# Two-layer diffusion backbone block: part of layer 0's gated convolution moved into the first attention block, and nine norm steps moved into the side queue

## The chip, the cores and the metric

The kernel runs on the 8 cores of one Trainium2 chip (trn2). Each pair of cores takes one batch item, each core one half of its 4096 positions (the second core of a pair in mirrored order), and every core runs the same program. The metric is the device time in microseconds of the slowest core.

## The reference

Layer 0 computes, from normalised and modulated tokens `xn`, a dense attention and a short gated convolution side by side, then one output projection, a residual add, a second norm and a SwiGLU feed-forward. Layer 1 is of the same build with windowed attention and a pooling mixer, which the change doesn't touch.

```python
q, k, v, gb, gc, u = split(xn @ w_in)                 # 1536, 512, 512, 512, 512, 512 columns
attn = dense_attention(rope(rms(q)), [kc; rope(rms(k))], [vc; v])   # 12 heads, 4352 keys
conv = gb * short_conv(gc * u, conv_w)                # depthwise, 3 taps, centred
y = concat([attn, conv]) @ w_out
h = h + gate1 * y
hn = rms_norm(h) * (1 + scale2) + shift2              # shift, scale, gate: c @ w_mod
h = h + gate2 * ((silu(hn @ w_gate) * (hn @ w_up)) @ w_down)
```

## The kernel before, in words

A core owns 2176 latent tokens and 256 context tokens, in the five token blocks of `QBLK`: blocks 0 to 3 of 512 tokens and block 4 of 384 (128 latent, 256 context; the gc and u products of block 4 take one more column, the neighbour token). The normalised tokens of the blocks lie in SBUF as `xnA[0]` to `xnA[4]`. Activations have features on the partitions, so a product of 128 output features over one block is 16 matmuls of 128x128 weights by up to 512 columns, summed in one PSUM bank.

The program writes out the order of every engine's instructions. `sc.op` appends to an engine's queue, with waits worked out from the slots that an instruction reads and writes; `sc.dma` appends a transfer to a queue (SP for data, POOL for weights); `sc.late` appends a store some operations later. All five queues run in order.

Weights stream through a ring of three slots (`NRING = 3`, `WStream`). The order of tiles is that of the `ws.take` calls. `ws.release` frees a slot, and `pump` then issues the load of the next tile in that order, which waits until TensorE has read the old one. So a tile is loaded when the tile three places ahead of it has been used, and never earlier. A tile of `w_mod` or `w_out` is 16x128x512 (float32 in HBM, bf16 in SBUF, 2048 KB there), one of `w_aux` (128 features of gb, gc and u) 1536 KB.

Layer 0 goes through these steps:

- `stage_a0`: norms, keys and values, then a list of items that `pipe` overlaps: 60 query items and, behind them, the items of `conv_items`. For each of four feature chunks `c` it takes the chunk's `w_aux` tile and makes gc, u (their product goes to the float32 row `zb`) and gb of all five blocks, 15 products; three taps over `zb` on VectorE, times gb, give the convolution, which is stored to `aux_d`. The products go round five PSUM banks; no other work runs beside them. Item `nq + 7` also keeps a `w_out` tile of layer 1: it is loaded through the ring and stored to `wo_d` by SP, and its slot is free after that store.
- `stage_b0`: attention. The query blocks go in the order `ORD[0]` = 0, 1, 2, 4, 3, called places p0 to p4 here. A place has 12 units (one head, 34 key tiles; p3 is built otherwise), a unit 17 groups of two key tiles. For each group `attn_gen` issues an exponential of 128x1024 on ScalarE, two score matmuls of the next group, two matmuls of the group before by the values, and the sums of the exponentials (VectorE adds and 5 matmuls per unit). A place of 512 queries is thus 204 groups.
- Behind each group, `side.weave` takes steps from a side queue. A group gives a credit of `rate` (2.5 times that for two groups of each unit), a step takes the cost that it yields. In p0 the rate is 0.105 and the queue holds `mod_gen` of the parts 2, 3 and 4 of the modulation: 12 tiles of `w_mod`, two steps per tile (a product of 16 matmuls and a copy; 4 float32 selections that the profile shows as 8 matmuls, and VectorE adds). In the places after it the queue holds `wout_gen`, the output projection of the place before (16 output chunks of 16 matmuls, in steps of 4), with `norm2_gen`, the second norm of the place before that (17 steps). Before a place begins, `side.drain` issues all that is left; the drain stands two groups ahead of the new place.
- `wout_last`: the last projection (p4), with nothing beside it. It issues the products of the first four output chunks, as far as the last heads are not needed, then all 17 steps of the norm of p3, then the loads of `hn` for the feed-forward (`load_hn`), then the rest. From step 28 on it takes one step of `xsum_gen` (VectorE sums for the feed-forward's products) per step of its own.
- The feed-forward, by Strassen-Winograd products (lines 1797 and 1944 of the profile).

Which lines are what in the profile: L593 is `mm`, thus every matmul but the feed-forward's; L1147 the exponential; L1150 the adds of exponentials; L610 the copy of a `mod_gen` tile; L671 and L683 the two operations of a norm step; L1412, L1421 and L1472 square, sum and residual add of `wout_gen`; L1700 the helper `tt` of the feed-forward; L195 and L199 every wait and every DMA.

## Time and profile before

| | us |
|---|---|
| Time, median of 3 runs | 6962.02 (6952.61 to 7265.59) |
| Profiled execution, its own time | 6981.62 |
| Its span, first to last instruction, slowest core (7) | 6980.1 |
| Spans of the eight cores | 6909.7 to 6980.1 |
| TensorE busy in that span | 6524.7 (93%) |
| VectorE / ScalarE busy | 3849.2 (55%) / 2389.2 (34%) |
| Convolution stage | about 732 to 933 |
| Places p0, p1, p2, p3, p4 | 933 to 1190, to 1458, to 1712, to 1884, to 2145 |
| Last projection, up to the feed-forward | 2145 to 2228 |

All rows are of core 7, times in microseconds from the start of its span. Busy time is that of instructions that compute; the granted clock (PEclk) is TensorE's, as a share of 2.4 GHz; the DMA share is the mean busy share of the core's 16 DMA engines. An entry in brackets behind a row of the timeline is the idle time of the engine ahead of it and what ended it.

### The profile page before, as it was taken

The numbers are of one execution on the slowest core, as the hardware profiler recorded it, in microseconds if no ns is written. First come the engines' busy times: TensorE is split into PE (matmuls) and PEld (weight loads), VectorE is DVE, ScalarE is ACT, GpSimd is POOL, SyncE is SP. The second block draws the span as 40 slices with busy tenths as digits, with TensorE's granted clock in tenths as the row PEclk, the third lists the DMA queues.
The fourth block names the chain that finished last, engine by engine and source line by source line (L and its number), as shares of the span: only waits on it lengthen the run. The fifth ranks groups of instructions, "written<-read, shape, count | busy, mean of one in ns | idle before, by whom it ended". The sixth has DMA issues, their size and how long they took to land.

```text
span 6980.1 us, 105992 instructions; the slowest of 8 cores (6909.7 to 6980.1 us)
## 1 busy us (share of the span) xinstructions
PE 6524.7 (93%) x35634; PEld 3401.5 (49%) x35634; DVE 3849.2 (55%) x6857; ACT 2389.2 (34%) x3782; POOL 225.3 (3%) x282
## 2 busy tenths in 40 slices
PE   2889999999897999999999999997989999999998
PEld 1334433433343665665675775453444444444443
DVE  1666445666666661663672663456766446374563
ACT  1666158787574110111220111555542001110111
POOL 0000000000000000000000000000000000000000
PEclk7999999999999999999999999998999999999999
DMA  9545576344747887777667868664576564866758
GB/s 184 145 125 116 109 154 125 86 107 114 180 99 162 131 135 179 111 124 184 131 113 173 138 110 211 136 122 136 206 211 115 123 137 86 201 128 150 156 106 175
DMA packets 470981, 983.07 MB, mean 141 GB/s; under 512 B 48688, under 2 KB 155952, under 8 KB 460464
## 3 DMA queue, kind: packets, MB, share of 16 engines
q0 software_dynamic: 228320, 517.78, 44.9%
q1 hardware_dynamic: 223120, 440.15, 19.8%
q10 hardware_dynamic: 19008, 18.35, 0.8%
q8 instruction: 295, 4.83, 0.3%
q14 instruction: 238, 1.95, 0.1%
HBM read 1275.47 MB, written 182.85 MB: 209 GB/s over the span
## 4 chain that ended last, share of the span: by engine, by line
PE 82%; DVE 5%; DMA 5%; ACT 4%; issue 3%; SPq 0%; another core or an unknown queue 0%; DVEq 0%; ACTq 0%; POOL 0%; POOLq 0%
PE pair L593 49%; PE pair L1797 32%; DMA arena<-w_mod 2%; DVE arena L1150 1%; ACT arena L1147 1%; DVE arena L1700 1%; ACT arena L683 1%; DVE arena L671 1%; PE pair L1289 1%; DMA hn<-arena 0%; DMA arena<-hn 0%; DMA q<-arena 0%; DMA arena<-w_down 0%; SPq L199 0%; DMA ud<-arena 0%
## 5 line engine op out<-in xcount | busy, mean ns | idle before, releaser
L593 PE MATMUL pair<-arena 128*128 128x512 bf16 (+6 forms) x20478 | 4111.6, 365 | 411.9 <-DMA arena<-w_mod 107.1
L593 PEld LDWEIGHTS pair<-arena 128*128 128x128 bf16 (+1 forms) x20478 | 1934.1, 101 | 2557.4 <-issue 814.5
L1797 PE MATMUL pair<-arena 128*128 128x320 bf16 (+2 forms) x14784 | 2398.8, 324 | 22.3 <-ACT arena L1810 10.0
L1797 PEld LDWEIGHTS pair<-arena 128*128 128x128 bf16 x14784 | 1441.6, 98 | 977.8 <-issue 63.2
L1700 DVE TENSOR_TENSOR arena<-arena,pair 128x320 f32<-128x320 f32 (+2 forms) x1584 | 861.0, 544 | 692.8 <-PE pair L1797 578.5
L1147 ACT ACTIVATE arena<-pair 128x1024 bf16<-128x1024 f32 (+2 forms) x896 | 867.0, 1001 | 199.7 <-PE pair L593 164.4
L1700 DVE TENSOR_TENSOR arena<-arena 128x1024 bf16<-128x1024 bf16 (+4 forms) x1224 | 789.9, 658 | 28.8 <-DMA arena<-hn 6.5
L1150 DVE TENSOR_TENSOR arena<-arena 128x1024 bf16<-128x1024 bf16 (+4 forms) x896 | 529.9, 600 | 425.1 <-ACT arena L1147 368.0
L1944 DVE SCALAR_TENSOR_TENSOR arena<-pair,arena 128x428 f32<-128x428 f32 (+3 forms) x320 | 202.0, 631 | 909.2 <-PE pair L593 873.1
L1810 ACT ACTIVATE arena<-pair 128x320 f32<-128x320 f32 (+2 forms) x264 | 125.0, 473 | 1566.0 <-PE pair L1797 1167.5
L671 DVE SCALAR_TENSOR_TENSOR arena<-arena 128x512 f32<-128x512 f32 (+6 forms) x448 | 280.3, 635 | 180.8 <-ACT arena L683 93.0
L683 ACT ACTIVATE arena<-arena 128x512 bf16<-128x512 f32 (+6 forms) x400 | 246.7, 617 | 190.7 <-DVE arena L671 130.3
L1803 ACT ACTIVATE arena<-arena 128x320 f32<-128x320 f32 (+2 forms) x264 | 136.1, 516 | 475.6 <-DVE arena L1700 475.6
L1803 ACT ACTIVATE arena<-pair 128x320 f32<-128x320 f32 (+2 forms) x264 | 127.4, 482 | 372.7 <-PE pair L1797 360.6
L1912 ACT ACTIVATE arena<-arena 128x428 f32<-128x428 f32 (+2 forms) x128 | 72.3, 564 | 476.0 <-DVE arena L1944 476.0
L775 DVE SCALAR_TENSOR_TENSOR arena<-pair,arena 128x512 f32<-128x512 f32 (+2 forms) x180 | 123.2, 684 | 135.0 <-ACT arena L770 131.6
L1472 DVE SCALAR_TENSOR_TENSOR arena<-pair,arena 128x512 f32<-128x512 f32 (+2 forms) x160 | 108.9, 683 | 119.4 <-PE pair L593 116.7
L759 ACT ACTIVATE arena<-pair 128x512 bf16<-128x512 f32 (+2 forms) x180 | 97.4, 541 | 202.8 <-PE pair L593 202.8
L1700 DVE TENSOR_TENSOR arena<-pair,arena 128x320 bf16<-128x320 f32 (+2 forms) x264 | 143.9, 545 | 24.0 <-PE pair L1797 22.1
L1256 ACT ACTIVATE arena<-pair 128x512 bf16<-128x512 f32 (+1 forms) x240 | 136.9, 593 | 54.3 <-PE pair L593 47.9
L790 DVE TENSOR_TENSOR arena<-pair,arena 128x512 f32<-128x512 f32 (+2 forms) x180 | 112.3, 624 | 72.4 <-PE pair L593 72.3
L199 POOL DMA_DIRECT2D arena<-w_gu x88 | 77.0, 875 | 2106.3 <-DVE arena L1700 1184.1
(69 smaller groups left out, 1884.4 us busy)
## 6 DMA issues: line engine op xcount, KB each, us to landing
arena<-w_gu POOLq DMA_DIRECT2D x88, 2048.0 KB, 17.4
arena<-w_down POOLq DMA_DIRECT2D x72, 1408.0 KB, 15.4
arena<-w_mod POOLq DMA_DIRECT2D x48, 2048.0 KB, 24.3
arena<-w_out POOLq DMA_DIRECT2D x24, 2048.0 KB, 20.5
arena<-w_in POOLq DMA_DIRECT2D x17, 2048.0 KB, 22.3
hT<-arena SPq DMA_DIRECT2D x32, 1024.0 KB, 15.6
arena<-wo POOLq DMA_DIRECT2D x16, 2048.0 KB, 10.6
arena<-x SPq DMA_DIRECT2D x56, 512.0 KB, 5.5
```

The source lines that it names most:

```text
L593: return e.matmul(out, lhsT=lhsT, rhs=rhs, start=start, stop=stop)
L671: sc.op("dve", lambda e, lo=lo, hi=hi, j=j: e.scalar_tensor_tensor(out=ta[:, lo:hi], in0=src[:, lo:hi], scalar=mcol(l, j, ps_, c), in1=rs[ ...
L683: sc.op("act", lambda e, lo=lo, hi=hi, j=j: e.activation(out=dst[:, lo:hi], in_=ta[:, lo:hi], func=AF.Identity, bias=mcol(l, j, pb_, c), s ...
L775: sc.op("dve", lambda e: e.scalar_tensor_tensor(out=tk[:, 0:n], in0=banks[pb][:, 0:n], scalar=dcol(gcol), in1=tr[:, 0:n], op0=ALU.mult, op ...
L1147: sc.op("act", lambda e: e.activation(out=dst, in_=src, func=AF.Exp, scale=float(ATT_SCALE)), reads=[s_bank[sb(gi, k)] for k in range(nb)] ...
L1150: sc.op("dve", lambda e, o=o, i0=i0, i1=i1: e.tensor_tensor(out=o, in0=i0, in1=i1, op=ALU.add), reads=rd, writes=[so])
L1256: sc.op("act", lambda e: e.activation(out=p[:, lo:512], in_=banks[bk][:, lo:512], func=AF.Exp, scale=float(ATT_SCALE)), reads=[s_bank[bk]] ...
L1700: sc.op("dve", lambda e: e.tensor_tensor(out=o, in0=i0, in1=i1, op=op), reads=rd, writes=wr)
L1797: ins = e.matmul(out, lhsT=A[:, k, :], rhs=B[k], start=start and k == 0, stop=k == 7, skip_group_check=True)
L1803: sc.op("act", lambda e: e.activation(out=o, in_=i, func=AF.Silu), reads=rd, writes=wr)
L1810: sc.op("act", lambda e: e.activation(out=w, in_=pc, func=AF.Copy), reads=[bc], writes=[sw])
L1944: sc.op("dve", lambda e, a=a, x0=x0, x1=x1, j=j, bk=bk, h=h, d=d: e.scalar_tensor_tensor(out=h[:, x0:x1], in0=banks[bk][:, x0 - a:x1 - a], ...
```

## The change

In `conv_items` only blocks 0 and 1 are left (6 products per chunk, 24 items). The convolution of block 1 stops two columns early, and the last columns of gb and of `zb` are kept in `sv`. The other blocks are made by the new generator `conv_gen(7)`, which is put at the head of the side queue in p0, ahead of the three `mod_gen`: for each chunk `c` it takes the `w_aux` tile a second time, holds it, and makes gc, u and gb of blocks 2, 3 and 4, 9 products, each in four steps of four matmuls that yield 1.0, 1.0, 1.0 and 1.3. All of them write bank 7. The rate of p0 goes from 0.105 to 0.78. The loads `load_Xb(0, 0)` and the aux part of the queries of p1 move from p0's second head group, and from ahead of the attention, to the start of p1. The buffers `zb2`, `cvt2`, `gcB`, `koB`, `sv` are new.

At p4 the first nine steps of the norm of p3 are put in the side queue behind the projection of p3. `wout_last` gets what is left of that generator (eight steps), and it begins the `xsum_gen` steps at step 24 instead of 28, for both layers.

```diff
...
+    sv, (s_sv,) = Region(BASE + 28336).take("sv", 20)
+    (zb2, (s_zb2,)), (cvt2, (s_cvt2,)) = (Region(BASE + o).take(nm, w) for o, nm, w in
+                                          ((25376, "zb2", 1420), (27820, "cvt2", 512)))
+    gcB, s_gcB = Region(BASE + 26796).take("gcB", 512, 2)
+    koB, s_koB = Region(BASE + 28448).take("koB", 256, 2)
+    koB = [bf(koB[:, 256 * i:256 * (i + 1)]) for i in range(2)]
...
-                f, bk, n = aproj(c, 0, b, False, b == 4)
+                f, bk, n = aproj(c, 0, b, False, b == 1)
...
+                    m = 512 - 2 * b
+                    taps(zb, s_zall, 1 + 512 * b, m, c, cvt, s_cvt)
...
+                    if b == 1:
+                        sc.op("act", lambda e: e.activation(out=sv[:, 5 * c:5 * c + 2], in_=banks[bk[0]][:, 510:512],
+                                                            func=AF.Copy), reads=[s_bank[bk[0]]], writes=[s_sv, s_bank[bk[0]]])
+                        sc.op("act", lambda e: e.activation(out=sv[:, 5 * c + 2:5 * c + 5], in_=zb[:, 1022:1025],
+                                                            func=AF.Copy), reads=[s_zall], writes=[s_sv])
+                    sc.late("sp", aux_d[c, :, a:a + m], ko[:, 0:m], f"{sko.name}", [sko], [sd(f"aux_{b}")])
                 items.append(dict(proj=f, s1=A))
             gcu(0)
-            for b in range(1, 5):
-                gcu(b)
-                gb(b - 1)
-            gb(4)
-
-
+            gcu(1)
+            gb(0)
+            gb(1)
+
+    def taps(z, s_z, zc, m, c, cv, s_cv, lo=0):
+        cw = V_CONV + 3 * c
+        o = cv[:, lo:lo + m]
+        sc.op("dve", lambda e: e.tensor_scalar(out=o, in0=z[:, zc:zc + m], scalar1=vcol(cw + 1), scalar2=None,
+                                               op0=ALU.mult), reads=[s_z, s_vecs], writes=[s_cv])
+        for d, w in ((-1, 0), (1, 2)):
+            sc.op("dve", lambda e, d=d, w=w: e.scalar_tensor_tensor(
+                out=o, in0=z[:, zc + d:zc + d + m], scalar=vcol(cw + w), in1=o, op0=ALU.mult, op1=ALU.add),
+                reads=[s_z, s_vecs, s_cv], writes=[s_cv])
+
+    def conv_gen(bk):
+        segs = {2: [(0, 512, 3)], 3: [(0, 512, 515)], 4: [(0, 128, 1027), (128, 384, 1157), (384, 385, 1155)]}
+        cnt = [0]
+        sc.op("dve", lambda e: e.memset(zb2[:, :], 0.0), writes=[s_zb2])
+        pb = banks[bk]
+        for c in range(4):
+            u = ws.take(waux[c])
+            wt = w16(u, 384)
+
+            def prod(which, b, n):
+                for kq in range(4):
+                    def f(e, kq=kq, wt=wt):
+                        for k in range(4 * kq, 4 * kq + 4):
+                            ins = mm(e, pb[:, 0:n], wt[:, k, 128 * which:128 * which + 128], xnA[b][:, k, 0:n],
+                                     k == 0, k == KD - 1)
+                        return ins
+                    sc.op("pe", f, reads=[s_ring[u], s_xnA[b]], writes=[s_bank[bk]])
+                    if kq < 3:
+                        yield 1.0
+
+            def conv(b):
+                n, a = QBLK[b][1], QBLK[b][0]
+                for lo, hi, zc in segs[b][:2]:
+                    taps(zb2, s_zb2, zc, hi - lo, c, cvt2, s_cvt2, lo)
+                ko, sko = koB[cnt[0] % 2], s_koB[cnt[0] % 2]
+                cnt[0] += 1
+                sc.op("dve", lambda e: e.tensor_tensor(out=ko[:, 0:n], in0=pb[:, 0:n], in1=cvt2[:, 0:n], op=ALU.mult),
+                      reads=[s_bank[bk], s_cvt2], writes=[sko])
+                sc.late("sp", aux_d[c, :, a:a + n], ko[:, 0:n], f"{sko.name}", [sko], [sd(f"aux_{b}")])
+
+            sc.op("act", lambda e, c=c: e.activation(out=zb2[:, 0:3], in_=sv[:, 5 * c + 2:5 * c + 5], func=AF.Copy),
+                  reads=[s_sv], writes=[s_zb2])
+            for b in (2, 3, 4):
+                n = QBLK[b][1] + (b == 4)
+                yield from prod(1, b, n)
+                g, s_g = gcB[:, 512 * (b % 2):512 * (b % 2) + n], s_gcB[b % 2]
+                sc.op("act", lambda e, g=g, n=n: e.activation(out=g, in_=pb[:, 0:n], func=AF.Copy),
+                      reads=[s_bank[bk]], writes=[s_g])
+                yield 1.3
+                yield from prod(2, b, n)
+                for lo, hi, zc in segs[b]:
+                    sc.op("dve", lambda e, lo=lo, hi=hi, zc=zc, g=g: e.tensor_tensor(
+                        out=zb2[:, zc:zc + hi - lo], in0=pb[:, lo:hi], in1=g[:, lo:hi], op=ALU.mult),
+                        reads=[s_bank[bk], s_g], writes=[s_zb2])
+                yield 1.3
+                if b == 2:
+                    taps(zb2, s_zb2, 1, 2, c, cvt2, s_cvt2)
+                    ko, sko = koB[cnt[0] % 2], s_koB[cnt[0] % 2]
+                    cnt[0] += 1
+                    sc.op("dve", lambda e, ko=ko, c=c: e.tensor_tensor(
+                        out=ko[:, 0:2], in0=sv[:, 5 * c:5 * c + 2], in1=cvt2[:, 0:2], op=ALU.mult),
+                        reads=[s_sv, s_cvt2], writes=[sko])
+                    sc.late("sp", aux_d[c, :, 1022:1024], ko[:, 0:2], f"{sko.name}", [sko], [sd("aux_1")])
+                else:
+                    yield from prod(0, b - 1, 512)
+                    conv(b - 1)
+                    yield 1.3
+            yield from prod(0, 4, 384)
+            ws.release(u)
+            conv(4)
+            yield 1.3
...
         xs = xsum_gen(l, 0)
         for k, _ in enumerate(wout_gen(l, p, nblk, (0, 1, 2, 3), prev, 0, True,
                                        lambda: load_hn(l, 0, (0, 4, 1, 5, 2, 6, 3, 7)))):
-            if k >= 28:
+            if k >= 24:
                 next(xs, None)
         for _ in xs:
             pass
...
             load_qa(0, 0, 0)
             return
         load_qa(0, 0, 1)
-        load_qa(0, 1)
-        steps = [iter(())]
+        load_qa(0, 1, 0)
+        steps, tail = [iter(())], [None]
         units = []
         for p, b in enumerate(ORD[0]):
             n = QBLK[b][1]
...
                 tiles = [(kv[:, 128 * t:128 * t + 128], kv[:, NALL + 128 * t:NALL + 128 * t + 128], None)
                          for t in range(NKT)]
                 kvs = [s_kvb[k % 2]]
-
-                def hook(k=k):
-                    kv_load(k + 1)
-                    if k == 1:
-                        load_Xb(0, 0)
+                hook = lambda k=k: kv_load(k + 1)
                 if b < 4:
                     for h in range(3 * g, 3 * g + 3):
                         new.append(dict(q=q[:, h, 0:n], qs=[s_q[h]], N=n, tiles=tiles, kvs=kvs,
...
                         new.append(dict(q=q[:, h, 128:384], qs=[s_q[h]], N=256, tiles=tiles[17:19],
                                         kvs=kvs, out=q[:, h, 128:384], outs=[s_q[h]]))
             for un in new:
-                un["rate"] = (0.105, 0.345, 0.4, 0.97, 0.4)[p]
+                un["rate"] = (0.78, 0.345, 0.4, 0.97, 0.4)[p]
             def start(p=p):
                 steps[0] = norm2_gen(0, p - 2, 5, 0.7, "dve") if p > 1 else iter(())
                 side.add(wout_gen(0, p - 1, 5, (7,), steps[0], 5))
+                if p == 4:
+                    tail[0] = norm2_gen(0, 3, 5, 0.7, "dve")
+                    side.add(itertools.islice(tail[0], 9))
             if p > 0:
-                new[0]["before"] = side.drain
+                new[0]["before"] = side.drain if p > 1 else lambda: (side.drain(), load_Xb(0, 0), load_qa(0, 1, 1))
                 new[0]["start"] = start
             units += new
+        side.add(conv_gen(7))
         for p in (2, 3, 4):
             side.add(mod_gen(0, p))
         side.weave(attn_gen(units, 2, (0, 1, 2, 3), (4, 5), 6), 1.0, 1.0)
         side.drain()
-        wout_last(side, 0, 4, 5, norm2_gen(0, 3, 5))
+        wout_last(side, 0, 4, 5, tail[0])
     def b1_loads():
         for t, (dst, s_) in enumerate(((kc1, s_kc1), (vc1, s_vc1))):
...
```

## Rows read from the trace of the kernel before

**Rows 1.** The page: busy time, share of the span and instructions.

```profile
PE 6524.7 (93%) x35634; PEld 3401.5 (49%) x35634; DVE 3849.2 (55%) x6857; ACT 2389.2 (34%) x3782; POOL 225.3 (3%) x282
```

**Rows 2.** Stretches: length, busy time of each engine (instructions), PEclk, DMA share, GB/s.

```profile
732.00:933.00 201.00, 201.00 (x971) 94.60 (x969) 82.41 (x140) 17.45 (x32) 4.34 (x6) 1.00 0.47 102
933.00:1190.00 257.00, 230.44 (x1166) 91.17 (x1166) 135.66 (x258) 218.24 (x240) 11.23 (x13) 1.00 0.84 160
1190.00:1458.00 268.00, 259.39 (x1139) 106.48 (x1137) 159.47 (x264) 214.21 (x231) 3.50 (x4) 0.99 0.38 89
1884.00:2145.00 261.00, 244.81 (x1121) 104.48 (x1120) 170.67 (x309) 208.78 (x225) 3.50 (x4) 0.98 0.38 91
2145.00:2205.00 60.00, 40.26 (x174) 17.41 (x172) 29.33 (x56) 21.50 (x44) 1.75 (x2) 0.83 0.89 233
```

**Rows 3.** Groups by form, PE, 732 to 933: shape, count, busy, mean ns, idle before.

```profile
L593 PE MATMUL pair<-arena 128*128 128x512 bf16 x777 | 171.3, 379 | 0.0
L593 PE MATMUL pair<-arena 128*128 128x385 bf16 x128 | 21.7, 326 | 0.0
L593 PE MATMUL pair<-arena 128*128 128x384 bf16 x66 | 11.7, 326 | 0.0
```

**Rows 4.** The same view, 933 to 1190.

```profile
L593 PE MATMUL pair<-arena 128*128 128x512 bf16 x878 | 212.2, 378 | 26.6 <-ACT arena L1147 17.4 <-DVE arena L1150 7.7
L593 PE MATMUL pair<-arena 128*32 128x512 bf16 x192 | 12.6, 381 | 0.0
L593 PE MATMUL pair<-arena 128*128 128x2 f32 x96 | 11.4, 240 | 0.0
```

**Rows 5.** The same view, 1190 to 1458.

```profile
L593 PE MATMUL pair<-arena 128*128 128x512 bf16 x1137 | 259.2, 382 | 8.6 <-ACT arena L1147 4.7 <-DVE arena L1150 2.3 <-DVE arena L1472 0.5
```

**Rows 6.** Timeline of ScalarE, 0 to 230: the copy behind a w_mod tile.

```profile
53.31 0.60 ACT L610 ACTIVATE arena<-pair 128x512 f32<-128x512 f32 x1 [11.88 <-PE pair L593]
65.03 0.60 ACT L610 ACTIVATE arena<-pair 128x512 f32<-128x512 f32 x1 [10.09 <-PE pair L593]
...
145.94 0.60 ACT L610 ACTIVATE arena<-pair 128x512 f32<-128x512 f32 x1 [8.08 <-PE pair L593]
```

**Rows 7.** Timeline of POOL, 600 to 1400: issues of ring loads.

```profile
783.13 1.64 POOL L199 DMA_DIRECT2D arena<-w_aux  x2 [50.19 <-DMA wo<-arena]
...
1047.54 0.87 POOL L199 DMA_DIRECT2D arena<-w_mod  x1 [19.45 <-PE pair L593]
```

**Rows 8.** DMA of 933 to 1190: the queue of ring loads (packets, MB, share of 16 engines).

```profile
q0 software_dynamic: 13520, 27.26, 67.2%
```

**Rows 9.** The page: the same queue over the whole span.

```profile
q0 software_dynamic: 228320, 517.78, 44.9%
```

**Rows 10.** Tile w_mod: who waited for its loads; and their landing.

```profile
PE pair L593: 107.1, 9
...
DMA to landing us min/median/max: 16.3/24.3/59.2
```

**Rows 11.** The DMA view: issues, KB each, us to landing.

```profile
arena<-w_aux POOLq DMA_DIRECT2D x4, 1536.0 KB, 14.4
```

**Rows 12.** Timeline of PE, 2125 to 2290.

```profile
2143.83 14.71 PE L593 MATMUL pair<-arena 128*128 128x512 bf16 x66 [0.68 <-DVE arena L1150]
2178.28 44.64 PE L593 MATMUL pair<-arena 128*128 128x512 bf16 x192 [19.74 <-DVE arena L1472]
```

**Rows 13.** Timeline of ScalarE, 2140 to 2240: norm steps.

```profile
2158.89 1.00 ACT L683 ACTIVATE arena<-arena 128x128 bf16<-128x128 f32 x2 [2.45 <-DMA hn<-arena]
...
2173.96 1.00 ACT L683 ACTIVATE arena<-arena 128x128 bf16<-128x128 f32 x2 [10.78 <-DMA hn<-arena]
```

**Rows 14.** Timeline of VectorE, 2140 to 2262: two halves of a norm step.

```profile
2176.53 0.94 DVE L671 SCALAR_TENSOR_TENSOR arena<-arena 128x128 f32<-128x128 f32 x2 [0.52 <-ACT arena L683]
```

**Rows 15.** Stretches with idle in them (columns as in rows 2).

```profile
2165.00:2178.00 13.00, 0.00 (x0) 0.00 (x0) 2.21 (x5) 3.11 (x7) 0.00 (x0) 0.50 1.02 206
2178.00:2205.00 27.00, 26.72 (x111) 11.55 (x112) 14.89 (x23) 6.62 (x12) 0.87 (x1) 0.90 1.01 300
```

More of the change, by code:

```diff
@@ L1 @@
+import itertools
 import numpy as np
@@ L965, in conv_items @@
     def conv_items(items):
-        zseg = {4: [(0, 128, 2049), (128, 384, 2179), (384, 385, 2177)]}
         cnt = [0, 0]
@@ L972, in aproj @@
             cnt[0] += 1
-            n = QBLK[b][1] + (1 if b == 4 and which else 0)
+            n = 512
             def f():
@@ L993, in zcols @@
         def zcols(b):
-            return zseg.get(b, [(0, 512, 1 + 512 * b)])
+            return [(0, 512, 1 + 512 * b)]
         for c in range(4):
@@ L1019, in A @@
                 def A():
-                    cw = V_CONV + 3 * c
-                    for (lo, hi, zc) in zcols(b)[:2]:
-                        m = hi - lo
-                        o = cvt[:, lo:hi]
-                        sc.op("dve", lambda e, o=o, zc=zc, m=m: e.tensor_scalar(
-                            out=o, in0=zb[:, zc:zc + m], scalar1=vcol(cw + 1), scalar2=None, op0=ALU.mult),
-                            reads=[s_zall, s_vecs], writes=[s_cvt])
-                        for d, w in ((-1, 0), (1, 2)):
-                            sc.op("dve", lambda e, o=o, zc=zc, m=m, d=d, w=w: e.scalar_tensor_tensor(
-                                out=o, in0=zb[:, zc + d:zc + d + m], scalar=vcol(cw + w), in1=o,
-                                op0=ALU.mult, op1=ALU.add), reads=[s_zall, s_vecs, s_cvt], writes=[s_cvt])
+                    m = 512 - 2 * b
@@ L1031, in A @@
+                    taps(zb, s_zall, 1 + 512 * b, m, c, cvt, s_cvt)
                     ko, sko = ix(TA, "ko", p)
-                    sc.op("dve", lambda e: e.tensor_tensor(out=ko[:, 0:n], in0=banks[bk[0]][:, 0:n], in1=cvt[:, 0:n],
+                    sc.op("dve", lambda e: e.tensor_tensor(out=ko[:, 0:m], in0=banks[bk[0]][:, 0:m], in1=cvt[:, 0:m],
                                                            op=ALU.mult),
                           reads=[s_bank[bk[0]], s_cvt], writes=[sko])
-                    sc.late("sp", aux_d[c, :, a:a + n], ko[:, 0:n], f"{sko.name}", [sko], [sd(f"aux_{b}")])
+                    if b == 1:
[3 more added lines that the diff above has]
+                                                            func=AF.Copy), reads=[s_zall], writes=[s_sv])
```

## The prediction

> **What bounds the kernel now.** First the page: TensorE is busy 93% of the span [rows 1], so time comes only from TensorE's idle stretches or from making new ones. Then the stretches [rows 2] around the change. In the convolution stage (732 to 933) TensorE has no idle time and the other engines are nearly free. In p0 it works 230.4 of 257 us beside ScalarE's 218.2; its 26.6 us of idle are put mostly on the exponentials [rows 4]: p0 is set by ScalarE and TensorE together, with 27 us of TensorE to be had. p1 shows what a place looks like when a side queue fills it: 8.6 us idle of 268 [rows 5]. The DMA share is 0.47 in the convolution stage, 0.84 in p0 and 0.38 in p1 [rows 2], because the 12 w_mod tiles are all loaded in p0. Between 2145 and 2205 TensorE works 40 of 60 us.
>
> **The products that move.** Per chunk six products of 512 columns and three of 384 or 385, times four chunks and 16 matmuls: 384 matmuls of 512 and 192 shorter ones. At the stage's own rates [rows 3], 384 x 171.3/777 = 84.7, and 21.7 + 64 x 11.7/66 = 33.0: the stage gets 117.7 us shorter, as nothing there hides it.
>
> In p0 they join 878 matmuls of attention and 24.0 us of modulation products (12.6 + 11.4) [rows 4]. A place with a full side queue takes 268/1139 = 0.235 us per matmul of 512, idle included [rows 2], since TensorE then sets the pace. So p0, were nothing else late, would take (878 + 384) x 0.235 + 192 x 0.181 (0.235 x 0.170/0.2205) + 24.0 = 355.8 us, 98.8 more than now. The net of moving is thus only -18.9 us. VectorE's part of the convolution (some 3/5 of the 82.4 us of the stage) and ScalarE's copies go beside that: 136 + 49 and 218 + 7 us in 356 [rows 2].
>
> **The turns on bank 7.** All 36 products use one bank, so each waits until ScalarE has copied or VectorE has read the one before. p1's projections in bank 7 do the same, and their waits are in its pace. New is that gc's copy stands between exponentials, and that ahead of the last product in a turn VectorE runs three taps of up to 0.75 us. I take 5 us; 0 if the 1.3 of credit covers it, 15 at 0.4 us per turn (VectorE adds cost TensorE 7.7 us in p0 now [rows 4]).
>
> **The modulation tiles.** This is the term that decides. conv_gen stands ahead of the three mod_gen, and the ring is in program order. I counted the credits: at 0.78 per group and 2.5-fold groups, conv_gen's 154.8 are used up behind group 171 of 204, and the 24 steps of mod_gen follow behind groups 171 to 196, ahead of the drain at 202. Now a tile is used about every 20 us [rows 7], which is why no load is waited for. After the change, until the last w_aux tile is released one of three slots is held, so just two w_mod tiles are in, and ten are still to load.
>
> What TensorE has to do in these 25 groups: 25 x 4.3 x 0.235 = 25.3, plus 24.0, is 49.3 us. What the loads need: 13 tiles (27.26 MB) took 67.2% of 257 us of all 16 engines, 13.3 us each [rows 8]; over the span 44.9% of 6980 for 517.8 MB is 12.7 us for 2.097 MB [rows 9]. At the kernel's start, where TensorE only waits for them (107.1 us, 9 times; shortest landing 16.3 [rows 10]), the copies behind the tiles come 11.7 us apart at best and 92.6/6 = 15.4 on average, with the loads of x beside them [rows 6]. So: first tile 16.3 us, nine more at 13.0, and 2 for the last tile's matmuls, 135.3 against 49.3. TensorE stands for 86 us. Ends: spacing 11.7 gives 74, spacing 15.2 gives 106. Attention can't go on meanwhile, for the matmuls of a mod_gen step stand in TensorE's queue ahead of the next group's, and ScalarE gets one group ahead at most.
>
> First the row, then a rule: a tile takes 13.3 us of the DMA engines [rows 8]. The Trainium skill ("DMA: Bandwidth & Descriptors", Specifications) gives some 358 GB/s as a core's limit on HBM. Taken on the 2.1 MB that land, an estimate by it is 5.9 us per tile, a stall of 22 and a sum of +3; taken on the 4.2 MB of float32 that are read it is 11.7 us and a sum of +55. The row lies by the second.
>
> **Around it.** The waits of other ring loads: w_aux of chunk 3 goes into the slot of the kept tile, whose store ended at 783.1 [rows 7] (its place in SP's queue is the same); with 14.4 us to land [rows 11] it is there at 797.5, wanted 18 products of 3.53 us behind 732, at 795.5: 3 us (0 to 8, if the next w_aux load shares the engines). Now it is wanted much later. The first w_out tile of p1 comes behind the last w_mod tile, 13 us later, and is wanted some 16 groups on: 2 us (0 to 6; load_Xb's 4 MB now share that moment). The four extra w_aux loads of 1.5 MB fall in 280 us in which the ring is full: nothing. SP's queue: kv_load waits as before, the moved load_Xb and aux loads stand at the start of p1, where p1's first 4 projection steps cover them. koB's stores are small, and SP is never waited for by its attention loads, that are made 51 groups ahead: nothing.
>
> **The clock.** In 13 us without a matmul it was granted at 0.50, and 0.90 over the 27 us after that [rows 15]. In the tile section TensorE works 49 of 135 us with waits of some 8 us, so I expect half clock in parts of it; even at twice the time, 98 us, its work fits beside the loads. What is left is the return to full clock: 3 us (0 to 10).
>
> **The nine norm steps.** Now TensorE works 14.7 us on the first chunks and then stands 19.7 us for L1472 [rows 12], which stands behind 16 norm steps on VectorE; these wait for the stores of hn to free their buffer, 10.8 us for the third [rows 13]. With nine steps done in p4, the two stores are long landed when the other eight begin: 8 x 1.1 us (a half pair takes 0.94 [rows 14], and the copy) from 2146.7 ends near 2156, ahead of TensorE's 2158.5. The whole 19.7 us goes. What is late next: the hn loads (5 MB), the last w_out tile, the stores of h and the first w_gu tile, all in a stretch whose DMA share is already 0.89 and, as it fills the wait, 1.02 [rows 2, 15]; I give back 6.7 of it, so -13 (-19.7 to 0). The nine steps cost p4 some 15 us of a VectorE that works 171 of 261 [rows 2]: nothing. xsum_gen starting four steps earlier shifts VectorE work beside TensorE: nothing, or part of the 6.7.
>
> **The sum** is -117.7 + 98.8 + 5 + 86 + 3 + 2 + 3 - 13 = +67.1 us. On the profiled execution's own 6981.6 (its span plus 1.5) that is 7048.7; the median of the runs is 19.6 below it, so I predict 7029.
>
> **Rivals.**
>
> (a) The tiles aren't waited for: the loads keep up with TensorE, as they do in all of p0 now. For it speaks that the trace shows no wait for w_mod outside the start, against it that the start is the one place where they were asked for faster than one in 13 us, and there each was waited for. Then the sum is 67.1 - 86 = -19, 6943. It decides if a tile takes less than 5.6 us: (49.3 + 19 - 16.3 - 2)/9 gives a sum of nothing. 10 in 100.
>
> (b) The turns on bank 7 cost much more: the taps and multiplication of gb, up to 2.7 us of VectorE behind its attention adds, and ScalarE's copies between exponentials hold TensorE at each turn for 1.5 us: 36 x 1.5 = 54 instead of 5, 7078. Against it: VectorE and ScalarE have a third of their time free in p0. 8 in 100.
>
> (c) The change doesn't do what it says: the rate leaves convolution steps for the drain, on TensorE alone. By my count the last is issued behind group 196. 2 in 100.
>
> **How the numbers follow.** 80 in 100 for the forecast; its own range, with stall and norm at their ends but not all at once, is 6995 to 7070. For 8 in 10 I go toward both rivals, 6980 to 7080. 2% of this kernel, about what a measurement can tell from no change, is 139 us: below 6823 nothing leads (1 in 100), above 7101 only (b) with long stalls (4), so within 2% 95.
>
> **What the changed profile would show.** The convolution stage some 84 us long (24 products); p0 some 440 us, with a DMA share near 1 and TensorE's busy share under 0.5 in its last 130 us before p1, and about ten waits for DMA w_mod that sum to 80 to 90 us; before that p0 as full as p1; the 19.7 us wait ahead of L1472 gone, with shorter waits at the start of the feed-forward. The prediction is wrong if the waits for w_mod are few, if p0's first 171 groups take over 1.75 us each, or if the last projection still stands for norm steps.

## The result, and the profile after

The changed kernel takes 1.0154 of the time before (95% interval 1.0125 to 1.0183), some 107 us more. It took 7071.6 and 7086.6 us, against 6952.6, 6962.0 and 6992.6 before; executions that fell in the chip's slower state, which both kernels have, are left out here and below. The profiled execution took 7071.58 us, its span on core 7 is 7070.0.

The prediction was 7029, in a range of 6980 to 7080: slower, by 67 us. The direction and the main term were right; the loss is 1.6 times what was forecast.

Where the time went shows best in stages, as means over the eight cores. The marks are the clearing of `zb` (the convolution stage begins), the first exponential, the first and the twelfth logarithm of a place (one closes each unit) and the first weight load of the feed-forward. Each is the start of an instruction in the view of its line, core by core.

| us, mean of 8 cores | before | after | change | forecast |
|---|---|---|---|---|
| convolution stage, to the first exponential | 199.1 | 94.4 | -104.7 | -114.7 |
| p0, to its last logarithm | 258.1 | 472.1 | +214.0 | +194.8 |
| p1 to p3, to p4's first logarithm | 708.7 | 708.4 | -0.3 | 0 |
| p4, first to last logarithm | 239.6 | 248.3 | +8.7 | 0 |
| last projection, to the feed-forward | 88.3 | 76.4 | -11.9 | -13 |
| sum | | | +105.8 | +67.1 |

The feed-forward begins 108.4 us later than before; the other 2.6 us stand ahead of the convolution stage.

First the busy times of the page (it answers to [rows 1]) and the waits of TensorE from the end of the convolution stage to the end of p0: who waited for whom, us in total, times, longest.

```profile
PE 6517.0 (92%) x35634; PEld 3405.4 (48%) x35634; DVE 3858.0 (55%) x6906; ACT 2379.4 (34%) x3762; POOL 228.6 (3%) x286
```

```profile
PE pair L600 <- DMA arena<-w_mod: 78.0, 10, 18.5
PE pair L600 <- DVE arena L1080: 18.4, 9, 3.7
PE pair L600 <- ACT arena L1218: 8.8, 12, 1.0
PE pair L600 <- DMA arena<-w_aux: 7.4, 1, 7.4
PE pair L600 <- DVE arena L1095: 5.2, 5, 1.7
```

Ten waits for w_mod, the ten tiles that were counted, 78 us. L600 is `mm`, L1218 the exponential, L1080 the multiplication of gb, L1095 that of gc and u: the last two free bank 7. As a mean of the eight cores the ten waits are 74.6 us. Now the timeline of TensorE at the end of p0, and that of POOL beside it (issues of ring loads).

```profile
1175.01 6.41 PE L600 MATMUL pair<-arena 128*32 128x512 bf16 x37 [18.54 <-DMA arena<-w_mod]
1189.35 7.37 PE L600 MATMUL pair<-arena 128*32 128x512 bf16 x33 [7.93 <-DMA arena<-w_mod]
1202.62 3.35 PE L600 MATMUL pair<-arena 128*32 128x512 bf16 x20 [5.89 <-DMA arena<-w_mod]
...
1292.18 10.29 PE L600 MATMUL pair<-arena 128*32 128x512 bf16 x49 [6.78 <-DMA arena<-w_mod]
```

```profile
1064.50 0.87 POOL L200 DMA_DIRECT2D arena<-w_mod  x1 [72.01 <-PE pair L600]
1143.40 0.87 POOL L200 DMA_DIRECT2D arena<-w_mod  x1 [78.02 <-PE pair L600]
1148.02 0.87 POOL L200 DMA_DIRECT2D arena<-w_mod  x1 [3.75 <-PE pair L600]
1153.92 0.87 POOL L200 DMA_DIRECT2D arena<-w_mod  x1 [5.03 <-PE pair L600]
1177.46 0.87 POOL L200 DMA_DIRECT2D arena<-w_mod  x1 [22.67 <-PE pair L600]
```

Between 1064.5 and 1143.4 nothing is loaded into the ring: it is full. Then a load is issued whenever a tile has been used, and TensorE waits for each. What is different from the forecast is the first: issued at 1143.4, used at 1175.0, 31.6 us later, not 16.3. SP's queue shows what shares the DMA engines with it; the last line is what that queue moved between 1143 and 1176 (packets, MB, share of 16 engines).

```profile
1109.37 0.32 SPq L200 DMA_DIRECT2D arena<-kT  x1
...
1146.77 2.39 SPq L200 DMA_DIRECT2D arena<-x  x4
1149.25 0.44 SPq L200 DMA_DIRECT2D arena<-aux  x1
```

```profile
q1 hardware_dynamic: 908, 4.49, 42.2%
```

The moved loads of `load_Xb` (4 MB) and of p1's aux part stand in the program at the start of p1, but SP's queue holds nothing that ties them to it. `Xb` lies where `xnA` lay, so they wait for the last read of `xnA`, and that is the end of the convolution, the moment at which the burst of tiles begins. The forecast had them behind the burst. Stretches, columns as in [rows 2]:

```profile
832.00:1150.00 318.00, 285.93 (x1335) 127.69 (x1336) 153.71 (x277) 189.60 (x210) 4.32 (x5) 0.98 0.28 65
1150.00:1308.00 158.00, 78.12 (x410) 35.23 (x411) 27.89 (x76) 38.83 (x46) 9.62 (x11) 0.65 1.06 182
```

The first part of p0 is filled at full clock with a DMA share of 0.28; the last 158 us have a share of 1.06 and TensorE half idle at a granted clock of 0.65, between the levels of 1.2 and 2.4 GHz. The w_mod tiles are the same twelve as before; they were only put into one stretch.

The last projection. TensorE's timeline answers to [rows 12]; VectorE's shows what it waits for at the end. L1543 is the residual add, L1492 the sum of squares, L1771 the feed-forward's helper, here the steps of `xsum_gen`.

```profile
2264.33 17.82 PE L600 MATMUL pair<-arena 128*128 128x512 bf16 x74 [1.95 <-ACT arena L1218]
2283.76 28.12 PE L600 MATMUL pair<-arena 128*128 128x512 bf16 x128 [1.61 <-DVE arena L1543]
2312.86 10.64 PE L600 MATMUL pair<-arena 128*128 128x512 bf16 x48 [0.97 <-DMA arena<-w_out]
2326.47 3.66 PE L600 MATMUL pair<-arena 128*128 128x512 bf16 x16 [2.97 <-DVE arena L1543]
2346.53 2.05 PE L600 MATMUL pair<-arena 128*128 128x512 f32 x2 [16.41 <-DVE arena L1492]
```

```profile
2329.33 0.82 DVE L1771 TENSOR_TENSOR arena<-arena 128x1280 bf16<-128x1280 bf16 x1 [3.01 <-DMA arena<-hn]
2336.74 1.56 DVE L1771 TENSOR_TENSOR arena<-arena 128x1280 bf16<-128x1280 bf16 x2 [6.58 <-DMA arena<-hn]
```

The 19.7 us of before are 1.6, and 16.4 us are new: the steps of `xsum_gen` stand on VectorE ahead of the last squares' adds and wait for the hn loads. That is the give-back that the forecast named, larger than its 6.7 us on this core; over all cores the stage is 11.9 us shorter, against 13.

And p4. ScalarE's timeline in its last unit (L1218 is the exponential, L686 the second half of a norm step, ACTq the issues of its DMA queue):

```profile
2241.58 3.91 ACT L1218 ACTIVATE arena<-pair 128x1024 bf16<-128x1024 f32 x4
2249.88 0.37 ACTq L200 DMA_DIRECT2D hn<-arena  x1
2250.46 1.94 ACT L1218 ACTIVATE arena<-pair 128x1024 bf16<-128x1024 f32 x2 [4.97 <-DVE arena L686]
...
2262.58 0.37 ACTq L200 DMA_DIRECT2D hn<-arena  x1
2263.16 1.94 ACT L1218 ACTIVATE arena<-pair 128x1024 bf16<-128x1024 f32 x2 [3.47 <-DVE arena L1221]
```

The nine steps fall in the last unit. A norm step costs more than VectorE time: each fourth ends in a store of hn that `hn_store` puts in ScalarE's queue. It waits for VectorE, and the exponentials of attention stand behind it, 5.0 and 3.5 us.

### The profile page after: what moved, and what is told of

Same layout as the page of the kernel before. It is cut to its first block, busy times and chain, and to the rows that moved or that the text cites. A ratio compares the mean times of both kernels' runs of the same rounds, so it can differ in the third digit from the quotient of the medians.

```text
span 7070.0 us, 105952 instructions; the slowest of 8 cores (7002.5 to 7070.0 us)
## 1 busy us (share of the span) xinstructions
PE 6517.0 (92%) x35634; PEld 3405.4 (48%) x35634; DVE 3858.0 (55%) x6906; ACT 2379.4 (34%) x3762; POOL 228.6 (3%) x286
## 4 chain that ended last, share of the span: by engine, by line
PE 81%; DMA 6%; DVE 5%; ACT 4%; issue 3%; SPq 0%; DVEq 0%; another core or an unknown queue 0%; ACTq 0%; POOL 0%; POOLq 0%
PE pair L600 48%; PE pair L1868 32%; DMA arena<-w_mod 4%; DVE arena L1221 1%; ACT arena L1218 1%; DVE arena L1771 1%; ACT arena L690 1%; DVE arena L678 1%; DMA arena<-hn 1%; PE pair L1360 0%; DMA ud<-arena 0%; DMA arena<-w_down 0%; DMA hn<-arena 0%; SPq L200 0%; DVE arena L1543 0%
## 5 line engine op out<-in xcount | busy, mean ns | idle before, releaser
L600 PE MATMUL pair<-arena 128*128 128x512 bf16 (+6 forms) x20478 | 4125.6, 368 | 509.0 <-DMA arena<-w_mod 185.3
L600 PEld LDWEIGHTS pair<-arena 128*128 128x128 bf16 (+1 forms) x20478 | 1948.3, 101 | 2653.3 <-issue 906.6
L1771 DVE TENSOR_TENSOR arena<-arena,pair 128x320 f32<-128x320 f32 (+2 forms) x1584 | 859.7, 543 | 681.2 <-PE pair L1868 567.4
L1218 ACT ACTIVATE arena<-pair 128x1024 bf16<-128x1024 f32 (+2 forms) x896 | 869.7, 1001 | 268.9 <-PE pair L600 223.5
L1771 DVE TENSOR_TENSOR arena<-arena 128x1024 bf16<-128x1024 bf16 (+4 forms) x1224 | 788.9, 657 | 42.1 <-DMA arena<-hn 19.7
L690 ACT ACTIVATE arena<-arena 128x512 bf16<-128x512 f32 (+4 forms) x368 | 232.1, 631 | 175.2 <-DVE arena L678 127.7
L1874 ACT ACTIVATE arena<-pair 128x320 f32<-128x320 f32 (+2 forms) x264 | 127.4, 482 | 371.0 <-PE pair L1868 359.0
L1543 DVE SCALAR_TENSOR_TENSOR arena<-pair,arena 128x512 f32<-128x512 f32 (+2 forms) x160 | 108.9, 682 | 111.9 <-PE pair L600 105.0
L1771 DVE TENSOR_TENSOR arena<-pair,arena 128x320 bf16<-128x320 f32 (+2 forms) x264 | 143.6, 544 | 21.6 <-PE pair L1868 19.0
L617 ACT ACTIVATE arena<-pair 128x512 f32<-128x512 f32 x48 | 28.7, 598 | 360.3 <-PE pair L600 360.3
## 6 DMA issues: line engine op xcount, KB each, us to landing
hT<-arena SPq DMA_DIRECT2D x32, 1024.0 KB, 14.1
```

The source lines that it names most:

```text
L600: return e.matmul(out, lhsT=lhsT, rhs=rhs, start=start, stop=stop)
L690: sc.op("act", lambda e, lo=lo, hi=hi, j=j: e.activation(out=dst[:, lo:hi], in_=ta[:, lo:hi], func=AF.Identity, bias=mcol(l, j, pb_, c), s ...
L1218: sc.op("act", lambda e: e.activation(out=dst, in_=src, func=AF.Exp, scale=float(ATT_SCALE)), reads=[s_bank[sb(gi, k)] for k in range(nb)] ...
L1771: sc.op("dve", lambda e: e.tensor_tensor(out=o, in0=i0, in1=i1, op=op), reads=rd, writes=wr)
L1874: sc.op("act", lambda e: e.activation(out=o, in_=i, func=AF.Silu), reads=rd, writes=wr)
```

## The experiments

Stages in us as means of the eight cores, and the ratio to the kernel before from runs beside each other. "p0" is to its last logarithm, as above.

| | conv. stage | p0 | p1 to p3 | p4 | last proj. | feed-forward begins | ratio (95% interval) |
|---|---|---|---|---|---|---|---|
| before | 199.1 | 258.1 | 708.7 | 239.6 | 88.3 | 2222.5 | |
| after | 94.4 | 472.1 | 708.4 | 248.3 | 76.4 | 2330.9 | 1.0154 (1.0125, 1.0183) |
| e1 | 94.3 | 368.6 | 704.4 | 248.8 | 78.3 | 2224.5 | 0.9998 (0.9983, 1.0013) |
| e2 | 94.8 | 471.2 | 706.5 | 238.8 | 88.3 | 2328.3 | 1.0169 (1.0139, 1.0198) |
| e3 | 199.2 | 258.1 | 705.7 | 249.0 | 76.6 | 2215.6 | 1.0007 (0.9962, 1.0051) |
| e4 | 94.3 | 404.9 | 706.5 | 248.1 | 76.8 | 2256.8 | 1.0052 (1.0028, 1.0077) |
| e5 | 95.3 | 358.0 | 707.8 | 248.8 | 79.0 | 2218.2 | none |
| e6 | 89.6 | 368.3 | 704.4 | 248.9 | 77.9 | 2216.8 | 0.9982 (0.9958, 1.0005) |
| e7 | 94.5 | 462.8 | 706.8 | 249.0 | 76.8 | 2317.2 | 1.0129 (1.0114, 1.0144) |
| e8 | 94.5 | 369.0 | 704.7 | 255.0 | 78.6 | 2230.7 | 1.0006 (0.9994, 1.0018) |
| e9 | 91.8 | 358.7 | 707.4 | 238.8 | 88.1 | 2214.3 | 0.9990 (0.9979, 1.0001) |
| e10 | 89.9 | 359.0 | 706.4 | 251.0 | 77.0 | 2211.6 | 0.9986 (0.9974, 0.9997) |
| e11 | 94.1 | 417.8 | 705.8 | 249.1 | 76.8 | 2271.9 | none |
| e12 | 93.3 | 369.0 | 701.0 | 243.9 | 75.7 | 2212.7 | 0.9985 (0.9973, 0.9998) |
| e13 | 88.7 | 359.0 | 702.5 | 243.2 | 76.3 | 2197.7 | 0.9989 (0.9972, 1.0006) |

Where nothing was changed, p0 and p4 repeat to about 1 us, the convolution stage and the last projection to 1 to 3, and p1 to p3 lie between 704.4 and 708.7. e5 and e11 have no ratio and are judged by their stages. In e5 and in the versions with its edit, lines behind the convolution have numbers 2 to 4 higher.

**e1, the tiles spread.** The change's `side.add(conv_gen(7))` and three `mod_gen` become one generator:

```python
def mixed(cg, mg, n=3):
    k = 0
    for w in cg:
        yield w
        if w == 1.3:              # a product is done, bank 7 is free
            k += 1
            if k % n == 0:
                for _ in range(2):
                    yield next(mg, None)
    yield from mg
```

> The changed kernel with one thing different: the two steps of each w_mod tile are put behind every third product of the woven convolution instead of behind all 36. A tile is then used about every 21 us again. Theory (the burst of tile loads makes the stall): the 78 us of waits for w_mod inside p0 go to under 5, TensorE keeps its full clock there, and the time is 1.004 of before (107 - 78 = +29 us). Rival (p0 is slow because convolution, modulation and attention crowd one another, whatever their order): the waits turn up elsewhere in p0 and the time stays at 1.012 or more.

Measured 0.9998. p0 is 103.5 us shorter than in the changed kernel and no wait for w_mod is left in it (waits of TensorE in p0, core 7):

```profile
PE pair L600 <- DVE arena L1080: 10.6, 9, 3.4
PE pair L600 <- ACT arena L1218: 9.9, 13, 1.0
PE pair L600 <- DVE arena L629: 5.6, 7, 1.4
PE pair L600 <- DVE arena L1095: 4.5, 4, 1.7
```

The burst was nearly the whole loss, and the rival falls. It cost more than its waits. As means of the cores the 103.5 us are 74.6 of waits for w_mod; 25.4 by which TensorE is busy longer with the same matmuls (363.3 against 337.9 us, at a granted clock over p0 of 0.87 against 1.00 on core 7); 8.6 of longer waits for L1080 and L1095 (23.6 against 15.0); and 5.0 less for L629, the adds of `mod_gen` (0.7 against 5.7).

**e7, the burst put first.** The `mod_gen` stand ahead of `conv_gen`.

> The changed kernel with the three mod_gen ahead of conv_gen in the side queue, so that the 24 steps come in a burst in p0's first groups. Theory (a burst of steps that each take a tile makes the stall, wherever it stands): waits for w_mod of about 100 us near p0's begin, p0 as long as in the changed kernel (430 to 450 us), 1.015 of before. Rival (only the place behind the held w_aux tile makes it, as one slot of the ring was taken): under 40 us of waits, 1.005.

Measured 1.0129, ten waits for w_mod of 77.4 us on the slowest core (not 100), p0 462.8. The place is not the cause. From the issue of the first of the ten loads to the last copy the burst takes 147.3 us here and 146.7 in the changed kernel (means of the cores). It is as long, though load_Xb isn't in it: on core 7 SP's queue moves 4.5 MB in it here (queries, keys and values for the most part), and 4.8 MB there. The first tile takes 22.4 us to its copy instead of 30.8, but the others come 13.9 us apart instead of 12.9. The 9.3 us by which p0 is shorter are at bank 7: the waits for L1080 and L1095 sum to 14.1 us instead of 23.6. Why they are shorter stays open.

**e11, half a burst.** `if k % n == 0 and k <= 18` in e1's generator: six tiles spread, six in a burst.

> A dose: six w_mod tiles behind every third product of the first 18 and six in a burst at the end, of which four are still to load. Theory (in a burst of n tiles the first to be loaded takes some 25 us and each next 13, against 4 us of work per tile): waits of about 35 us, and p0 some 45 us longer than the interleaved 337.6, thus 378 to 388. Rival (the wait for loads isn't proportional, a burst costs its start or nothing): under 350 or over 420.

p0 is 49.2 us longer than e1's (386.8 from first to last logarithm, in the range), with four waits that sum to 45.0 us on the slowest core (some 35 were expected), the longest 21.8. Half the tiles cost half the loss, and the first of a burst costs the most.

**e4, tiles of half the bytes.** `ws.take(wo_d[t])` in place of the w_mod tile; the kernel then leaves out the true modulation parts 2 to 4.

> The changed kernel, but the 12 modulation tiles of p0 are read from bf16 tiles in HBM (the kept output weights of layer 1) instead of the float32 w_mod, so the modulation parts 2 to 4 of layer 0 are computed from other weights. The same 2 MB land, half as many bytes are read and nothing is converted. Theory (a tile's 13 us are set by the float32 bytes read): the spacing of the tiles falls to 6 to 8 us, the waits from 78 to about 20 us, and the time to 1.007 of before. Rival (bytes that land, or a fixed cost per tile, set it): the waits stay above 65 us and the time at 1.015.

The copies behind the third and the twelfth tile, in the changed kernel and in e4 (a fence each):

```profile
1177.07 0.60 ACT L617 ACTIVATE arena<-pair 128x512 f32<-128x512 f32 x1 [21.11 <-PE pair L600]
...
1294.24 0.60 ACT L617 ACTIVATE arena<-pair 128x512 f32<-128x512 f32 x1 [10.06 <-PE pair L600]
```

```profile
1155.30 0.60 ACT L617 ACTIVATE arena<-pair 128x512 f32<-128x512 f32 x1 [4.35 <-PE pair L600]
...
1220.01 0.60 ACT L617 ACTIVATE arena<-pair 128x512 f32<-128x512 f32 x1 [2.09 <-PE pair L600]
```

Nine intervals of 13.0 us there, of 7.2 here, with the same 2 MB landing. So neither the bytes that land nor a fixed cost per tile set the pace; the rival falls. The edit halves the bytes read and also takes away the conversion from float32, and these two weren't separated. The Trainium skill ("DMA: Bandwidth & Descriptors", Specifications) gives 358 GB/s as a core's limit on HBM; an estimate by it on the 4.2 MB that are read is 11.7 us, and the trace has 13.0 (323 GB/s). The 7.2 us are a bound from above, as here only five to seven of the ten tiles were waited for, 14.4 us in all on the slowest core. Yet p0 is 36.3 us longer than e1's. As means of the cores, 14.1 of them are these waits, 14.7 are longer busy time of TensorE for the same matmuls (352.6 against 337.9 us), with the clock low as in the changed kernel, and 8.2 are longer waits for L1080 and L1095 (23.2 against 15.0); the rest are small waits in both directions.

```profile
1160.00:1180.00 20.00, 12.97 (x81) 5.35 (x73) 4.36 (x11) 5.88 (x7) 1.06 (x2) 0.76 1.01 335
```

**e2 and e3, the norm part undone and alone.** e2 is the changed kernel with all 17 norm steps in the last projection again; e3 the kernel before with

```python
if p == 4:
    tail[0] = norm2_gen(0, 3, 5, 0.7, "dve")
    side.add(itertools.islice(tail[0], 9))
```

> The changed kernel with the norm part undone: all 17 norm steps again inside the last projection, xsum from step 28. Theory (the gain of the gone 19.7 us wait is given back, as the hn loads hold VectorE, and p4 pays 6 us): 5 us faster to 0 slower than the changed kernel, 1.015 of before, with the 19.7 us wait for the residual add back and the 16.4 us wait for the sum of squares gone. Rival (the prediction's term, -13 us, holds and something else hides it): 13 us slower than the changed kernel, 1.017.

> The kernel before with the norm part alone: nine norm steps in the side queue of p4, xsum from step 24. Theory: p4 6 us longer, the last projection 2 us shorter, together +4 us, 1.0006 of before. Rival (the prediction's term): 13 us faster, 0.998.

Both agree to a microsecond: the move makes the last projection 11.9 to 11.7 us shorter (88.3 to 76.4 undone in e2, 88.3 to 76.6 in e3) and p4 9.5 to 9.4 us longer. Together -2, which no ratio can show. My theory's two sizes (p4 +6, last projection -2) came from core 7, whose last projection was the shortest of the eight before; the forecast's -13 was the better figure for that stage.

**e8 and e10, why p4 pays.** e8 is e1 with p4's rate 0.46 instead of 0.4; e10 has that rate too, the nine steps cost 2.1 instead of 0.7 in it, and it has e5's and e6's edits.

> The interleaved version with the side rate of p4 at 0.46 instead of 0.40, so that the nine norm steps (their VectorE halves are 15 us) are issued over more groups and end ahead of the last unit. Theory (p4's +10 us comes from nine steps packed into the last unit, where VectorE holds the attention): p4 falls from 248.8 to 240 to 244 us and the time to 0.999 of before. Rival (the steps cost p4 their VectorE time wherever they stand): p4 stays at 247 to 250.

> The same three, with the norm part kept, its nine steps at a cost of 2.1 instead of 0.7 and p4's rate 0.46, so that a step stands behind every fourth or fifth group instead of two behind three. Theory (p4's +10 us comes from the density: 1.7 us of VectorE per step between groups of 1.15 us): p4 is 240 to 245 us instead of 248.8, the last projection stays at 77 and the time is 0.9965 of before. Rival (p4 is short of VectorE or TensorE time wherever the steps stand): p4 at 248 or more.

p4 grew to 255.0 in e8 and is 251.0 in e10. By p4 alone both theories fall, but both versions also changed the rate, so p4 has to be read in two parts: the first eight of its eleven intervals between logarithms, and the last three, in which all nine steps stand (means of the cores).

| us | first eight | last three |
|---|---|---|
| before | 176.3 | 63.3 |
| e1 | 175.4 | 73.3 |
| e8 | 182.3 | 72.7 |
| e10 | 182.1 | 68.9 |
| e12 | 173.7 | 70.2 |

The nine steps cost 10.0 us. In e8 they stand in the two intervals ahead of the last one, which is back at 19.1 us; those two take 26.5 and 27.1 instead of 21.7 and 22.5, and the sum of the three stays: packing into the last unit is not the cause. In e10 the three are 4.4 us shorter than in e1: density is a part of it. What made p4 longer all the same is the rate, 6.7 to 6.9 us in the first eight intervals, where none of the nine steps stands. e10 is 0.14% faster than the kernel before, not the 0.35% expected.

**e12, the store moved.** e1 with

```diff
-            sc.late("act", hn_d[d - 3:d + 1, ...
+            sc.late("sp" if l == 0 else "act", hn_d[d - 3:d + 1, ...
```

> The interleaved version with layer 0's stores of hn issued from SP's queue instead of ScalarE's. Theory (p4's +10 us is two stores in ScalarE's queue that wait 5.0 and 3.5 us for the norm steps on VectorE, with the exponentials behind them): p4 falls from 248.8 to 240 to 242 us, the last unit from 28.9 to about 21, the waits of ScalarE for L686 to nothing; 0.9985 of before. Rival (VectorE's 15 us of norm work is what costs): p4 stays at 247 or more.

p4 is 243.9 instead of 248.8, between theory and rival; p1 to p3 are 701.0 instead of 704.4 (their norm steps have such stores too), the waits of ScalarE for L686 are gone, 0.9985. Of the 4.9 us in p4, 3.1 are in the last three intervals, where the nine steps stand; 1.8 are in the fifth (21.3 instead of 23.1), whose stores the kernel before has too. So the nine steps' stores in ScalarE's queue are some 3 of their 10 us. The rest stays, with the VectorE work as what is left to explain it, which was not isolated.

**e5, the taps ahead.** e1 with the three taps of gb's product emitted ahead of the product.

> The interleaved version (w_mod tiles behind every third product), and the three taps of each gb product are put ahead of the product instead of between it and the multiplication that frees bank 7. Theory (VectorE's taps hold the bank at each gb turn): the 10.6 us of waits for that multiplication in p0 go to under 3, p0 is 5 to 8 us shorter than the interleaved 337.6, 0.999 of before. Rival (the turns are bound by the attention's own pace): p0 stays within 3 us.

p0 is 10.6 us shorter (358.0 against 368.6; 5 to 8 were expected), the waits for the multiplication 2.3 us instead of 10.6:

```profile
PE pair L600 <- ACT arena L1222: 10.1, 13, 1.1
PE pair L600 <- DVE arena L629: 5.3, 7, 1.4
PE pair L600 <- DVE arena L1097: 4.1, 4, 1.6
PE pair L600 <- DVE arena L1082: 2.3, 3, 1.1
```

**e6, the kept tiles early.** e1 with `items[(12, 32, 46, 54)[t]]["pre"] = keep`.

> The interleaved version, with the four kept w_out tiles at query items 12, 32, 46 and 54 instead of the last at item 67, so that the fourth w_aux tile doesn't wait for the kept tile's store. Theory: the 7.4 to 7.8 us wait for w_aux goes, with it the half clock behind it, and the convolution stage is 84 us long instead of 94.5, which makes 0.9985 of before. Rival (the ring is late anyway, since w_aux loads share the DMA engines with the first keys and queries): the wait stays above 4 us or moves to another tile.

The wait for w_aux is gone, but the stage only falls from 94.3 to 89.6: on five of the eight cores TensorE then waits once for 4.1 to 5.8 us for ScalarE's copies into `sv`, on the others up to 1.4. The wait moved, though not to another tile as the rival had it, and about half of the term was to be had.

**e9 and e13, versions put together.** e9: e1, e5, e6, norm part undone. e13: e1, e5, e6 and e12.

> Interleaved tiles, taps ahead of gb's products and the early kept tiles together, with the norm part of the change undone. The terms measured one by one: against the interleaved version (1.000 of before) 10.6 us less in p0, 4.7 less in the convolution stage, and the norm's -2 given up: -13 us, 0.998 of before. Rival (p0 then waits elsewhere, as one core in three did when the w_aux wait went): 1.000.

> The interleaved version with the three measured repairs: taps ahead of gb's products (-10.6 in p0), the kept tiles early (-4.7 in the convolution stage), stores of hn from SP (-8 in p4 if the run beside it shows that). Theory: 6910 to 6920, 0.9965 of before, faster than e10. Rival (the terms don't add, as in e9, where p0 and the stage fell by 12.4 us and the time by 0.1%): 0.999.

e9 0.9990, halfway between its theory and its rival, e13 0.9989, its rival's; both have an interval that contains 1. In e13's profile the feed-forward begins 24.8 us earlier than before, mean of the cores, yet its executions took 6911.3 to 6956.6 us (median 6926.3) beside 6933.5 to 6945.7 (median 6937.2): 11 us, with more spread. The layers behind the change take 4688 to 4719 us by core in one profile, and the slowest core counts. Why little of the lead arrives at the end is open. No version beats the kernel before by more than 0.2%.

## Why the prediction was right in part, and where it failed

- **The products that move** (-117.7 in the stage, +98.8 in p0, net -18.9): e1 measures the move without the burst: -104.8 in the stage and +110.5 in p0, net +5.7. The halves came out worse by 12.9 and 11.7 us, of which the sum had 3 and 5 in terms of their own: the w_aux wait was 7.4 us on core 7 instead of 3, with the clock at 0.91 over 800 to 900, and the turns cost more. This net is why the change couldn't gain, whatever the tiles did. TensorE's 27 us of idle in p0 weren't filled: in e1 they are 30.7 (368.6 less 337.9 busy), of them 15.0 for L1080 and L1095, 5.7 for `mod_gen`'s adds and 8.6 for the exponentials.
- **The turns on bank 7** (+5): mis-sized. The waits for L1080 and L1095 are 23.6 us in the changed kernel, 15.1 in e1; the taps alone are worth 10.6 us (e5). Rival (b) had the mechanism at 54.
- **The modulation tiles** (+86, with +3 for the clock and +2 for w_out): the mechanism is shown by e1, e7, e11 and e4. Ten waits and the spacing of 13.0 us came as worked out. The loss was 103.5 instead of 91, and 11.4 of the 12.5 us are the length of the burst: 135.3 us in the prediction, 146.7 measured from the first load's issue to the last copy (mean of the cores; 150.8 on core 7). The step that failed is the first tile's 16.3 us. It came from the kernel's start, and load_Xb was placed at the start of p1, behind the burst, so nothing was left to share the DMA engines. The trace has load_Xb inside: the first tile took 31.6 us on core 7. That step looked at the place in the program, not at what SP waits for. Which loads they are matters less than that there are some: e7's burst, with 4.5 MB of others, is as long.
- **The work beside the loads**: "even at twice the time, 98 us, its work fits beside the loads" held. The work took 72.1 us (146.7 - 74.6) instead of 49.3, and each of the ten tiles was still waited for. That the waits, 74.6, came near the 86 is thus in part luck: the burst was longer than worked out, and so was the work in it.
- **The w_aux wait**: right place, 7.4 us instead of 3.
- **The nine norm steps**: -13 in the last projection was right (-11.9). That the nine steps cost p4 "nothing" failed by 9.5 us. The step had set their 15 us of VectorE against VectorE's idle share of the whole place, though they stand in its last units, and hadn't counted the stores that a norm step issues in ScalarE's queue, some 3 us of it by e12.
- **What would show it**: the DMA share near 1, TensorE's busy share under 0.5 in the burst and the ten waits for w_mod came as listed, with 74.6 us for 80 to 90. The stage of 84 us came as 94 and p0's 440 as 472. Ahead of the burst p0 wasn't as full as p1: TensorE is busy for 0.90 of 832 to 1150, against 0.97 in p1 [rows 2]. Its first 171 groups took 308.8 us (mean of the cores), 1.81 each, over the 1.75 that the prediction named as a sign of being wrong; the turns on bank 7 stand there. Rival (a) fell: each of the ten was waited for. So did rival (c): the copy of the last tile stands behind exponential 195 of 204, where the count had group 196.

By size of error: the burst 12.5 us, the stage 10.0, p4 8.7, the turns and pace of p0 6.7, the last projection 1.1; together with p1 to p3 (-0.3) these are the 38.7 us between +67.1 and +105.8.

## What to carry to other kernels

Work that takes a weight tile must be spread by the time that a tile's load takes, not by the credit that its instructions cost: with a ring of three, everything that stands at the end of a side queue behind a long holder arrives as a burst, and n tiles there cost (n - 2) loads, with whatever else is loaded in that moment, less the work between them. When a step is moved, follow every DMA that it issues into the queue that issues it, and ask what stands behind it there and what its wait is really tied to; a queue with nothing to wait for runs ahead of its place in the program. Idle time of an engine is worth moving work into only by what the moved work's own turns leave of it: here p0, with 27 us of idle, took in 107 us of TensorE's work (busy 230.9 before, 337.9 in e1) and grew by 110.5.

## What the runs showed of the hardware

A ring load of 2 MB of bf16 from float32 took 13.0 us per tile with loads back to back; from bf16 the tiles came 7.2 us apart, with not every one waited for. A burst cost more than its waits: TensorE was busy 25.4 us longer with the matmuls of p0 in the changed kernel and 14.7 us longer in e4 than in e1, with the granted clock at 0.65 in the burst (1150 to 1308 in the changed kernel) and 0.76 in e4's (1160 to 1180), where TensorE worked about half of the time or more. Two stores in ScalarE's queue, waiting for VectorE, held the exponentials behind them for 5.0 and 3.5 us.
